# A decoder trunk on one core: the last block of a projection taken half by half, and the norm's reciprocal and spread in two pieces

## The chip, the core and the metric

The kernel runs on one core of a Trainium2 chip. The metric is the device time of one launch in microseconds. 2992.96 us is the median of 3 runs of the kernel before.

## What is computed

A step of a four-layer decoder trunk over 512 prompt tokens and 8 sample tokens, 520 columns in all, with a model width of 1024. Each layer has a token mixer (a gated short convolution, RWKV-7, gated linear attention, a short convolution again) and a gated feed-forward part with a convolution. Each of these eight sub-layers stands between two norms:

```
def rmsnorm(x, g, eps=RMS_EPS):
    xf = x.astype(jnp.float32)
    y = xf * lax.rsqrt(jnp.mean(xf * xf, axis=-1, keepdims=True) + eps)
    return (y * g.astype(jnp.float32)).astype(x.dtype)
...
        u = rmsnorm(h, p['norm_g'][l, 0]) * (1 + sc_m) + sh_m
...
        h = h + gt_m * rmsnorm(out, p['norm_g'][l, 1])
        u = rmsnorm(h, p['norm_g'][l, 2]) * (1 + sc_f) + sh_f
        out, nb = conv_ffn(u, st_conv_f[l], p['ffn_w_up'][l], p['ffn_conv_w'][l], p['ffn_conv_b'][l],
                           p['ffn_w_down'][l])
        new_f.append(nb)
        h = h + gt_f * rmsnorm(out, p['norm_g'][l, 3])
```

That is sixteen norms: eight ahead of a sub-layer (here "pre") and eight behind it ("post").

## The kernel before

Activations lie transposed: the 1024 features are eight tiles of 128 partitions, the 520 tokens are the columns. A projection is a row of blocks, each one output tile of 128 features. A block's accumulator `tile_ps[slot]` is two PSUM banks, one for each half of 260 tokens. Weights are split into a high and a low part so that products keep float32 accuracy: for each block SyncE loads `w_raw`, ScalarE writes `w_hi` (`high`, L1037), GpSimd writes `w_lo` (`low`, L814), and TensorE (`gemm`) takes, for all k, `w_hi` with the high and the low part of x (L1722), both halves in turn, and then, for all k, `w_lo` with the high part (L1730). It waits for `lo_done` only between the two. Two weight slots alternate, and `high` for a block waits until the block two before it is done. A block of the out phase has 8 tiles of k, 48 matmuls; a down block is three pieces with 8, 7 and 7 (`DOWN_K`), the last with 42.

The projections `out` and `down` end in a post norm. During them VectorE squares each finished tile and adds it up in `csb[:, 0]`; `sum_ready` says that all tiles but the last are in it. The last tile is squared by ScalarE straight from PSUM (`square_last`, L1100 and L1101, one instruction for a half), after the whole block is done, and then copied (`evacuate`, L1106, L1107). TensorE adds over features with a matrix of ones (`token_sums`, L1784), first `csb[:, 0]` and then the squares of the last tile. The result has 4 groups of rows, with 128 prompt columns each, and 8 sample columns: 136 columns. ScalarE takes the root (`root`, L1063), VectorE the reciprocal (`inverse_root`, L2641), and TensorE spreads it over all partitions (`spread_rstd`): L1826 is one product for the 8 sample columns, L1828 four products of 128 columns, float32. Each of these is two weight loads and two matmuls in the trace. VectorE then multiplies the eight tiles by it (`times_rstd`, L2695) and adds to `h` (L2751).

A pre norm squares `h` tile by tile on ScalarE (L1072) as the post norm finishes it, and goes on with the same root, reciprocal and spread. Of its eight, seven follow a post norm at once; the first is in the prologue, where TensorE also works on loads of `ada_pro`.

In six of the eight posts TensorE has other work, the modulation products of the next half layer (`ada_ahead`, L1683): four steps, 32 instructions, between `token_sums` and `spread_rstd`, and four more after. The posts at 2566 and 2971 us have none. All engines run queues in program order and wait for each other by semaphores, whose counts are written out by hand.

Of the kernel before, what the change touches and what calls it, by code (L numbers as in the profile page):

```python
# [16 lines left out]
ACT = mybir.ActivationFunctionType  # L17
# [7 lines left out]
HALF = T // 2  # L25
KT = D // P
DFF = 2816
FT = DFF // P
# [20 lines left out]
NG = 4  # L49
TG = T // NG  # L50
SPAN = 3 * TG
NW = TP // NG
# [19 lines left out]
def trunk_kernel(nc, A, O, depth):  # L72

    ctx = ExitStack()
    with ctx:
# [194 lines left out]
        def sem(name):  # L270
            return ctx.enter_context(nc.semaphore(name))
# [35 lines left out]
        usb_done = sem("usb_done")  # L307
        uhi_done, last_squared = sem("uhi_done"), sem("last_squared")
        u_ready = sem("u_ready")
        h_ready = sem("h_ready")  # L310
# [708 lines left out]
        def _(act):  # L1019
# [76 lines left out]
            def square_last(s, n, index):  # L1096

                act.wait_ge(sum_ready, index + 1)
                act.wait_ge(block_done, n + 3)
                act.activation(csb[:, 1, 0:HALF], tile_ps[s][0][:, 0:HALF], ACT.Square)  # L1100
                act.activation(csb[:, 1, HALF:T], tile_ps[s][1][:, 0:HALF], ACT.Square).then_inc(last_squared, 1)  # L1101
# [546 lines left out]
        def _(pe):  # L1648
# [65 lines left out]
            def gemm(n, s, slot, xh, xl, k0, nk, start, stop, ready=None, between=None):  # L1714
# [17 lines left out]
                return mm.then_inc(block_done, 1)  # L1732

            def gemm_pair(n, pre, xh, xl, ready, hi=(uhi_done, None), weights=(w_hi, w_lo), start=True, stop=True):

# [86 lines left out]
            def spread_rstd(norm):  # L1822

                pe.wait_ge(rstd_ready, norm + 1)
                row = lambda g: ident[:, g * QUAD:g * QUAD + 1].to_broadcast([P, P])
                pe.matmul(rstd_ps[1], row(NG - 1), rstd[:, NW:NGW], start=True, stop=True).then_inc(rstd_turned, 1)  # L1826
                for g in range(NG):
                    mm = pe.matmul(rstd_ps[0][:, g * NW:(g + 1) * NW], row(g), rstd[:, 0:NW], start=True, stop=True)  # L1828
                mm.then_inc(rstd_turned, 1)
# [27 lines left out]
            for p in plan:  # L1857
# [632 lines left out]
                elif p["kind"] == "out":  # L2490
                    xh, xl, ready, r0 = p["x"]

                    def out_block(it, e):

                        pe.wait_ge(tile_free[e], t0 // 2 + it + 1)
                        gemm(n0 + 2 * it + e, e, e, xh, xl, 0, KT, True, True, (ready, r0) if e == 0 else None)

# [13 lines left out]
                    if l % 3 == 2:  # L2511
                        for b in range(2 * p["iters"]):
                            out_block(b // 2, b % 2)
                            if b < NS // 2:
                                sample_products(b)
                    else:
                        first = 0
                        if l % 3 == 0:
                            out_block(0, 0)
                            turn_tails(p["conv"])  # L2520
                            out_block(0, 1)
                            first = 1
                        with pe.Fori(first, p["iters"]) as it:
                            for e in range(2):
                                out_block(it, e)
                elif p["kind"] == "up":
                    pe.wait_ge(std_done, p["norm"])
# [18 lines left out]
                elif p["kind"] == "down":  # L2546
# [3 lines left out]
                    def down_pair(it):  # L2550
                        for e in range(2):
                            pe.wait_ge(tile_free[e], t0 // 2 + it + 1)
                            for i, (k0, nk) in enumerate(DOWN_K):
                                k = 3 * e + i
                                gemm(n0 + 6 * it + k, k % 2, e, hid_hi, hid_lo, k0, nk, i == 0, i == 2,
                                     (hid_ready, p["unit"] - FT + k0) if e == 0 else None)
                                if it == 0 and k == 1:
# [27 lines left out]
        def _(dve):  # L2585
# [52 lines left out]
            def inverse_root(norm):  # L2638

                dve.wait_ge(std_done, norm + 1)  # L2640
                dve.reciprocal(rstd[:, 0:NGW], std[:, 0:NGW]).then_inc(rstd_ready, 1)  # L2641

# [624 lines left out]
```

## Time and profile before

| what | value |
|---|---|
| median of 3 runs | 2992.96 us (2991.05 to 2993.82) |
| the profiled execution | 2992.34 us |
| its span, first to last instruction | 2990.5 us |
| TensorE matmuls busy | 2845.7 us, 95% |
| weight loads busy | 2711.8 us, 91% |
| VectorE, ScalarE, GpSimd busy | 51%, 36%, 44% |
| mean granted TensorE clock | 0.975 of full |
| reciprocals L2641 | 16, 1.00 us each |

The busy shares are means over stages with different limits. For this change the stages between two projections matter, and there the order of starts in the timeline says who waits for whom. Matmuls are pipelined: each is shown some 0.27 us long while they follow each other every 0.11 to 0.12 us, so the distance between starts is what a matmul costs. For the weight loads (PEld) the same holds.

### The profile page before, as it was taken

The numbers are of one execution on the slowest core, as the hardware profiler recorded it, in microseconds if no ns is written. First come the engines' busy times: TensorE is split into PE (matmuls) and PEld (weight loads), VectorE is DVE, ScalarE is ACT, GpSimd is POOL, SyncE is SP. The second block draws the span as 40 slices with busy tenths as digits, with TensorE's granted clock in tenths as the row PEclk, the third lists the DMA queues.
The fourth block names the chain that finished last, engine by engine and source line by source line (L and its number), as shares of the span: only waits on it lengthen the run. The fifth ranks groups of instructions, "written<-read, shape, count | busy, mean of one in ns | idle before, by whom it ended". The sixth has DMA issues, their size and how long they took to land. (4 is left out here: it accounts for less than half of the span.)

```text
span 2990.5 us, 71312 instructions
## 1 busy us (share of the span) xinstructions
PE 2845.7 (95%) x29353; PEld 2711.8 (91%) x29353; DVE 1535.0 (51%) x2080; ACT 1062.6 (36%) x2047; POOL 1314.5 (44%) x957
## 2 busy tenths in 40 slices
PE   6999999998998999899999899999999999899998
PEld 5998999997988986899998799889999899799998
DVE  3445766117446885676603342476650444577612
ACT  3224333225455652433323543343332422433322
POOL 3443544442434563354443273434444344355443
PEclk8999999998999999999999999999999999899999
DMA  7544333444411004333344323533334543233332
GB/s 268 166 149 171 92 91 91 157 128 135 121 51 31 4 12 136 123 91 91 104 157 154 112 64 113 171 120 91 91 116 149 172 125 86 64 91 91 90 93 86
DMA packets 462286, 332.59 MB, mean 111 GB/s; under 512 B 16567, under 2 KB 432261, under 8 KB 461791
## 3 DMA queue, kind: packets, MB, share of 16 engines
q1 hardware_dynamic: 460148, 325.80, 35.2%
q10 hardware_dynamic: 1930, 3.68, 0.5%
q8 instruction: 172, 2.82, 0.4%
q14 instruction: 36, 0.29, 0.0%
HBM read 319.66 MB, written 10.20 MB: 110 GB/s over the span
## 5 line engine op out<-in xcount | busy, mean ns | idle before, releaser
L814 POOL TENSOR_TENSOR w_lo<-w_raw,w_hi 128x1024 fp32r<-128x1024 f32 x394 | 1005.0, 2551 | 1095.3 <-ACT w_hi L1037 1074.7
L1722 PE MATMUL banks<-u_hi,w_hi 128*128 128x260 f32 x4016 | 812.6, 283 | 18.9 <-ACT w_hi L1037 18.9
L1722 PE MATMUL banks<-u_lo,w_hi 128*128 128x260 f32 x4016 | 812.1, 283 | 0.0
L1722 PEld LDWEIGHTS banks<-u_hi,w_hi 128*128 128x128 f32 x4016 | 620.5, 189 | 29.4 <-issue 24.3
L1722 PEld LDWEIGHTS banks<-u_lo,w_hi 128*128 128x128 f32 x4016 | 621.6, 189 | 0.0
L1037 ACT ACTIVATE w_hi<-w_raw 128x1024 fp32r<-128x1024 f32 x402 | 424.6, 1057 | 463.9 <-PE banks L1730 296.7
L1730 PE MATMUL banks<-u_hi,w_lo 128*128 128x260 f32 x4016 | 520.7, 282 | 0.0
L1730 PEld LDWEIGHTS banks<-u_hi,w_lo 128*128 128x128 f32 x4016 | 497.0, 188 | 0.0
L1722 PE MATMUL banks<-hid_hi,w_hi 128*128 128x260 f32 x1664 | 336.4, 283 | 0.5 <-DVE hid_lo L2683 0.5
L1722 PE MATMUL banks<-hid_lo,w_hi 128*128 128x260 f32 x1664 | 335.1, 283 | 0.0
L3202 DVE TENSOR_TENSOR csb<-proj 128x520 f32 (+1 forms) x42 | 30.2, 719 | 470.2 <-ACT proj L1107 470.2
L2683 DVE TENSOR_TENSOR hid_lo<-prod,hid_hi 128x520 f32 x104 | 262.0, 2520 | 12.8
L1722 PEld LDWEIGHTS banks<-hid_hi,w_hi 128*128 128x128 f32 x1664 | 256.7, 188 | 5.7 <-issue 3.7
L1722 PEld LDWEIGHTS banks<-hid_lo,w_hi 128*128 128x128 f32 x1664 | 256.1, 188 | 0.0
L2667 DVE SCALAR_TENSOR_TENSOR conv<-gate,vecs,conv 128x536 f32<-128x536 f32 x104 | 246.9, 2374 | 15.1 <-DVE conv L2665 0.8
L1730 PE MATMUL banks<-hid_hi,w_lo 128*128 128x260 f32 x1664 | 217.0, 282 | 0.0
L1730 PEld LDWEIGHTS banks<-hid_hi,w_lo 128*128 128x128 f32 x1664 | 206.4, 188 | 0.0
L832 POOL TENSOR_TENSOR tails<-gate,ones 128x2 f32 (+1 forms) x104 | 29.2, 281 | 328.9 <-ACT gate L1595 328.9
L1602 ACT ACTIVATE conv<-conv,vecs 128x536 f32<-128x536 f32 x88 | 65.5, 744 | 288.2 <-DVE conv L2667 288.2
L1593 ACT ACTIVATE gate<-banks 128x260 f32<-128x260 f32 x88 | 34.1, 387 | 356.4 <-PE banks L1730 355.7
L2664 DVE TENSOR_SCALAR conv<-gate,vecs 128x536 f32<-128x536 f32 x104 | 57.9, 556 | 177.0 <-ACT gate L1595 173.0
L2665 DVE SCALAR_TENSOR_TENSOR conv<-gate,vecs,conv 128x536 f32<-128x536 f32 x104 | 113.8, 1095 | 15.2 <-DVE conv L2664 1.6
(471 smaller groups left out, 3840.0 us busy)
## 6 DMA issues: line engine op xcount, KB each, us to landing
w_raw<-in_ffn_w_up_dram SPq DMA_DIRECT2D x176, 512.0 KB, 3.7
ada_raw<-in_ada_w_dram SPq DMA_DIRECT2D x96, 512.0 KB, 4.7
w_raw<-in_ffn_w_down_dram SPq DMA_DIRECT2D x64, 448.0 KB, 3.7
w_raw<-in_sconv_w_in_dram SPq DMA_DIRECT2D x48, 512.0 KB, 5.0
ada_ahead<-in_ada_w_dram SPq DMA_DIRECT2D x36, 512.0 KB, 7.2
ada_ahead_down<-in_ada_w_dram SPq DMA_DIRECT2D x36, 512.0 KB, 5.9
w_raw<-in_ffn_w_down_dram SPq DMA_DIRECT2D x32, 512.0 KB, 4.0
ada_pro<-in_ada_w_dram SPq DMA_DIRECT2D x6, 2048.0 KB, 21.5
```

The source lines that it names most:

```text
L814: pool.tensor_tensor(w_lo[:, s, :, :], w_raw[:, s, :, :], w_hi[:, s, :, :].bitcast(F32), ALU.subtract).then_inc(lo_done, 1)
L832: pool.tensor_tensor(to[:, 0:2], gate[:, e, TP:TP + 2], ones[:, 0:2], ALU.mult).then_inc(pool_step, 1)
L1037: act.activation(w_hi[:, s, :, :], w_raw[:, s, :, :], ACT.Copy).then_inc(hi_done, 1)
L1593: act.activation(gate[:, e, 2:2 + HALF], tile_ps[0][0][:, 0:HALF], ACT.Copy)
L1602: act.activation(conv[:, e, 0:CWD], conv[:, e, 0:CWD], ACT.Silu, bias=vec("ffn_conv_b", l * FT + m)).then_inc(silu_done, 1)
L1722: pe.matmul(tile_ps[slot][half][:, 0:HALF], w_hi[:, s, k, :], x[:, k0 + k, half * HALF:(half + 1) * HALF], start=start and k == 0 and i == ...
L1730: mm = pe.matmul(tile_ps[slot][half][:, 0:HALF], w_lo[:, s, k, :], xh[:, k0 + k, half * HALF:(half + 1) * HALF], start=False, stop=stop an ...
L2664: link(dve.tensor_scalar(conv[:, e, 0:CWD], gate[:, e, 0:CWD], w[0], None, ALU.mult))
L2665: link(dve.scalar_tensor_tensor(conv[:, e, 0:CWD], gate[:, e, 1:1 + CWD], w[1], conv[:, e, 0:CWD], ALU.mult, ALU.add))
L2667: dve.scalar_tensor_tensor(conv[:, e, 0:CWD], gate[:, e, 2:2 + CWD], w[2], conv[:, e, 0:CWD], ALU.mult, ALU.add).then_inc(conv_done, 1)
L2683: dve.tensor_tensor(lo, prod[:, e, :], hi.bitcast(F32), ALU.subtract).then_inc(hid_ready, 1)
L3202: return dve.tensor_tensor(csb[:, 1, :], o, o, ALU.mult)
```

## The change

The last block of an `out` or `down` projection is computed by a new function, `gemm_halves`: all products of the first half of tokens, then all of the second. It waits for `hi_done` and `lo_done` before its first matmul. A new semaphore, `first_half_done`, is raised between the halves, and `square_last` squares the first half on it. The loops over output tiles run one iteration less on TensorE and the last one is written out. The reciprocal becomes two instructions, columns 64 to 135 first and then 0 to 63, and the four products of L1828 become eight with 64 columns each, the upper columns first, behind a wait for their piece.

```
             def square_last(s, n, index):
                 act.wait_ge(sum_ready, index + 1)
+                act.wait_ge(first_half_done, index + 1)
+                act.activation(csb[:, 1, 0:HALF], tile_ps[s][0][:, 0:HALF], ACT.Square)
                 act.wait_ge(block_done, n + 3)
-                act.activation(csb[:, 1, 0:HALF], tile_ps[s][0][:, 0:HALF], ACT.Square)
                 act.activation(csb[:, 1, HALF:T], tile_ps[s][1][:, 0:HALF], ACT.Square).then_inc(last_squared, 1)
...
+            def gemm_halves(n, s, slot, xh, xl, k0, nk, start):
+
+                pe.wait_ge(hi_done, n + 1)
+                pe.wait_ge(lo_done, n + 3)
+                for half in range(2):
+                    for k in range(nk):
+                        for w, x in ((w_hi, xh), (w_hi, xl), (w_lo, xh)):
+                            mm = pe.matmul(tile_ps[slot][half][:, 0:HALF], w[:, s, k, :],
+                                           x[:, k0 + k, half * HALF:(half + 1) * HALF],
+                                           start=start and k == 0 and w is w_hi and x is xh, stop=k == nk - 1 and w is w_lo)
+                    mm.then_inc(block_done if half else first_half_done, 1)
...
             def spread_rstd(norm):
-                pe.wait_ge(rstd_ready, norm + 1)
+                pe.wait_ge(rstd_ready, 2 * norm + 1)
                 row = lambda g: ident[:, g * QUAD:g * QUAD + 1].to_broadcast([P, P])
                 pe.matmul(rstd_ps[1], row(NG - 1), rstd[:, NW:NGW], start=True, stop=True).then_inc(rstd_turned, 1)
-                for g in range(NG):
-                    mm = pe.matmul(rstd_ps[0][:, g * NW:(g + 1) * NW], row(g), rstd[:, 0:NW], start=True, stop=True)
+                for part in (1, 0):
+                    pe.wait_ge(rstd_ready, 2 * norm + 2 - part)
+                    cols = slice(part * NW // 2, (part + 1) * NW // 2)
+                    for g in range(NG):
+                        out = rstd_ps[0][:, g * NW:(g + 1) * NW]
+                        mm = pe.matmul(out[:, cols], row(g), rstd[:, cols], start=True, stop=True)
                 mm.then_inc(rstd_turned, 1)
...
-                    def out_block(it, e):
+                    def out_block(it, e, final=False):
                         pe.wait_ge(tile_free[e], t0 // 2 + it + 1)
-                        gemm(n0 + 2 * it + e, e, e, xh, xl, 0, KT, True, True, (ready, r0) if e == 0 else None)
+                        if final and e:
+                            gemm_halves(n0 + 2 * it + e, e, e, xh, xl, 0, KT, True)
+                        else:
+                            gemm(n0 + 2 * it + e, e, e, xh, xl, 0, KT, True, True, (ready, r0) if e == 0 else None)
...
-                        with pe.Fori(first, p["iters"]) as it:
+                        with pe.Fori(first, p["iters"] - 1) as it:
                             for e in range(2):
                                 out_block(it, e)
+                        for e in range(2):
+                            out_block(p["iters"] - 1, e, True)
...
+                                if it == p["iters"] - 1 and k == 5:
+                                    gemm_halves(n0 + 6 * it + k, k % 2, e, hid_hi, hid_lo, k0, nk, False)
...
             def inverse_root(norm):
                 dve.wait_ge(std_done, norm + 1)
-                dve.reciprocal(rstd[:, 0:NGW], std[:, 0:NGW]).then_inc(rstd_ready, 1)
+                dve.reciprocal(rstd[:, NW // 2:NGW], std[:, NW // 2:NGW]).then_inc(rstd_ready, 1)
+                dve.reciprocal(rstd[:, 0:NW // 2], std[:, 0:NW // 2]).then_inc(rstd_ready, 1)
```

(`NG` is 4, `NW` 128, `NGW` 136, `HALF` 260.)

## Rows read from the trace of the kernel before

**Rows 1.** The page, parts 1 and 4 (busy time; chain that ended last)
```profile
PE 2845.7 (95%) x29353; PEld 2711.8 (91%) x29353; DVE 1535.0 (51%) x2080; ACT 1062.6 (36%) x2047; POOL 1314.5 (44%) x957
...
PE banks L1722 24%; PE banks L1730 12%; PE banks L2055 1%; PE banks L1683 1%; DVE h L2751 1%; PE banks L1745 1%; DVE proj L2695 1%; PE banks L1828 0%; PE banks L1784 0%; PE banks L1751 0%; PE banks L2006 0%; PE banks L2116 0%; PE banks L213
```

**Rows 2.** Timeline, post norm at 257: start, length, engine, line, operation, [idle before]
```profile
252.06 0.70 DVE L3228 TENSOR_TENSOR csb<-csb 128x520 f32<-128x520 f32 x1
...
256.43 0.39 ACT L1100 ACTIVATE csb<-banks 128x260 f32<-128x260 f32 x1 [4.19 <-PE banks L1730]
...
256.71 0.38 ACT L1101 ACTIVATE csb<-banks 128x260 f32<-128x260 f32 x1
...
257.14 0.44 PE L1784 MATMUL banks<-csb,ones 128*32 128x136 f32 x8 [0.45 <-ACT csb L1101]
...
257.40 1.91 PE L1683 MATMUL banks<-ada_ahead,cT 128*32 128x256 f32 x32
...
257.65 0.37 ACT L1063 ACTIVATE std<-banks,eps_col 128x136 f32<-128x136 f32 x1
...
258.13 1.00 DVE L2641 RECIPROCAL rstd<-std 128x136 f32<-128x136 f32 x1
...
259.24 0.30 PEld L1826 LDWEIGHTS banks<-rstd,ident 128*128 128x128 f32 x2 [0.41 <-DVE rstd L2641]
...
259.46 0.97 PEld L1828 LDWEIGHTS banks<-rstd,ident 128*128 128x128 f32 x8
...
260.73 1.29 DVE L2695 TENSOR_TENSOR proj<-proj,banks 128x512 f32<-128x512 f32 x2 [0.19 <-PE banks L1828]
```

**Rows 3.** Timeline of the pre norm at 274, TensorE and VectorE
```profile
274.58 0.39 PE L1826 MATMUL banks<-rstd,ident 128*128 128x8 f32 x2 [1.54 <-DVE rstd L2641]
...
276.05 0.69 DVE L2695 TENSOR_TENSOR prod<-h,banks 128x512 f32<-128x512 f32 x1 [0.83 <-PE banks L1828]
```

**Rows 4.** Timeline of the post norm at 2566, TensorE
```profile
2567.48 0.39 PE L1826 MATMUL banks<-rstd,ident 128*128 128x8 f32 x2 [1.60 <-DVE rstd L2641]
```

**Rows 5.** Timeline of the pre norm at 2581, weight loads of the spread
```profile
2582.45 1.83 PEld L1828 LDWEIGHTS banks<-rstd,ident 128*128 128x128 f32 x8
```

**Rows 6.** Windows: stretch, length, busy us of each engine, PEclk, DMA share, GB/s
```profile
2580.90:2590.10 9.20, 6.70 (x30) 6.38 (x31) 6.13 (x13) 4.79 (x8) 0.00 (x0) 0.50 0.01 2
...
2970.70:2972.40 1.70, 0.13 (x1) 0.13 (x2) 1.23 (x2) 0.41 (x2) 0.00 (x0) 1.00 0.00 0
```

**Rows 7.** Timeline: low parts of two last blocks, and the blocks before them
```profile
1204.75 2.90 POOL L814 TENSOR_TENSOR w_lo<-w_raw,w_hi 128x1024 fp32r<-128x1024 f32 x1 [2.83 <-ACT w_hi L1037]
...
1206.57 2.07 PE L1730 MATMUL banks<-u_hi,w_lo 128*128 128x260 f32 x16
...
2960.60 2.40 POOL L814 TENSOR_TENSOR w_lo<-w_raw,w_hi 128x1024 fp32r<-128x1024 f32 x1 [2.57 <-ACT w_hi L1037]
...
2962.55 1.83 PE L1730 MATMUL banks<-hid_hi,w_lo 128*128 128x260 f32 x14
```

**Rows 8.** Timeline of the post norms at 670 and 1942
```profile
668.35 1.06 ACT L1037 ACTIVATE w_hi<-w_raw 128x1024 fp32r<-128x1024 f32 x1 [9.86 <-DMA w_raw<-in_rwkv_w_dram]
...
1942.03 0.94 DVE L2739 TENSOR_TENSOR s<-proj_b,mod_m 128x64 f32<-128x64 f32 x1 [4.91 <-ACT proj_b L1107]
...
1944.06 0.39 PE L1826 MATMUL banks<-rstd,ident 128*128 128x8 f32 x2 [0.48 <-DVE rstd L2641]
```

**Rows 9.** Groups by line: two reciprocals; timeline: loads of L2055
```profile
L2641 DVE RECIPROCAL rstd<-std x16: 1002/1003/1005, 31.8 to 2971.2; 128x136 f32<-128x136 f32 x16
...
L3131 DVE RECIPROCAL rstd<-std x1: 966/966/966, 1138.6 to 1138.6; 128x130 f32<-128x130 f32 x1
...
1741.87 2.42 PEld L2055 LDWEIGHTS banks<-g_ex 128*128 128x128 f32 x21
```

**Rows 10.** Timeline of the prologue, TensorE
```profile
44.88 3.64 PE L1849 MATMUL banks<-ada_pro,cT 128*32 128x128 f32 x64 [3.28 <-DMA ada_pro<-in_ada_w_dram]
```

**Rows 11.** The core's span and mean granted clock
```profile
core 0: 2990.5 us, clock 0.975
```

More of the change, by code:

```diff
@@ L308, in trunk_kernel @@
         uhi_done, last_squared = sem("uhi_done"), sem("last_squared")
+        first_half_done = sem("first_half_done")
         u_ready = sem("u_ready")
@@ L2512, in _ @@
                         for b in range(2 * p["iters"]):
-                            out_block(b // 2, b % 2)
+                            out_block(b // 2, b % 2, b == 2 * p["iters"] - 1)
                             if b < NS // 2:
@@ L2554, in down_pair @@
                                 k = 3 * e + i
-                                gemm(n0 + 6 * it + k, k % 2, e, hid_hi, hid_lo, k0, nk, i == 0, i == 2,
-                                     (hid_ready, p["unit"] - FT + k0) if e == 0 else None)
+                                if it == p["iters"] - 1 and k == 5:
+                                    gemm_halves(n0 + 6 * it + k, k % 2, e, hid_hi, hid_lo, k0, nk, False)
+                                else:
+                                    gemm(n0 + 6 * it + k, k % 2, e, hid_hi, hid_lo, k0, nk, i == 0, i == 2,
+                                         (hid_ready, p["unit"] - FT + k0) if e == 0 else None)
                                 if it == 0 and k == 1:
```

## The prediction

> **What bounds the kernel now.** I read the page first. TensorE is busy for 95% of the span and the weight loads beside it for 91%, while no other engine passes 51%; the chain that ended last runs over L1722 and L1730, the projection matmuls [rows 1]. Time is made or lost where TensorE starves, and the norms are such places. So I then read the stages around the norms in the timeline, one by one; this change touches nothing else.
>
> A post norm begins when the last block of a projection ends. In the pattern that four posts show (at 257, 1215, 1624 and 2353 us) the reader should follow ScalarE first [rows 2]: the two squares start at 256.43 and 256.71, then two copies, then the root at 257.65. ScalarE works without a gap here, and TensorE's sums end at 257.58, so both allow the root at about the same moment. Then come the reciprocal (258.13 to 259.13), the small product L1826 at 259.24 and the eight loads of L1828 from 259.46. In these posts TensorE has 32 instructions of L1683 between sums and spread; they end about 259.3, so L1826 starts behind them, not behind the reciprocal, which was there some 0.05 us before. L2695 at 260.73, and all of the norm behind it, waits for L1828.
>
> A pre norm has nothing on TensorE between sums and spread: it idles 1.54 us for the reciprocal, L1826 starts at 274.58 and L2695 at 276.05 [rows 3]. Seven pres are on the path, six of them like this. The post at 2566 has no L1683 either, and idles 1.60 us [rows 4]; the post at 2971 is like it up to L1826. Two spreads met the lower level of the clock: from 2580.9 to 2590.1 the granted clock was 0.50, 1.2 GHz, and there the eight loads of L1828 took 1.83 us instead of 0.97; in the post at 2971 it was full until 2972.4 and half behind that, with L1828 wholly in the lower part [rows 2, 5, 6].
>
> **The wait for w_lo.** The last block now asks for w_lo before its first matmul. In an out phase w_lo is there at 1207.65 and the block before ends its matmuls at about 1208.6; in a down phase it is there at 2963.00, and the block before ends at 2964.4 [rows 7]. So 0.9 to 1.4 us of TensorE's work on the previous block hides it: 0; without that cover it would cost the 2.4 to 2.9 us of a low part. The order of the 48 (or 42) matmuls changes, not their number, and each already has a weight load of its own, so the block stays as long. That the last iteration leaves the loop costs nothing either: TensorE shows no idle time between two blocks in a loop or out of it.
>
> **The early square.** sum_ready comes at 252.76 [rows 2], the first half of the block is done halfway through its 5.7 us, at about 253.5, and ScalarE is free by then. The first square moves under the second half, and the second starts at 256.43 instead of 256.71. Copies, root, sums and L1683 all come 0.28 us earlier. This holds in seven of eight posts. At 670 both squares stand behind a w_hi that its DMA kept until 668.35, after the block's end: nothing there. In the post at 1942 VectorE's small multiply takes 0.94 us, to 1942.97, beside a low part of POOL that is not moved, and the reciprocal starts only behind it: nothing there [rows 8]. Six times 0.28 is -1.68 us.
>
> **The reciprocal in two pieces.** 136 columns take 1003 ns and 130 take 966 [rows 9]: 6.2 ns for a column and a fixed 0.16 us. The first piece, 72 columns, then takes about 0.606 us, the second 0.557, and L1826 can start 0.397 us earlier, where it waits for the reciprocal. It does in the seven pres, in the posts at 2566 and 2971, and in those at 670 and 1942, where the reciprocal starts late (L1826 at 1944.06, while L1683 had ended some 0.5 us before): 11 times -0.397 is -4.37 us. In the four posts of rows 2 L1683 hides it: 0. If a piece had no fixed part the gain would be 0.8 us more. The second piece ends about 1.2 us after the root, and the first eight loads run until 1.8, so its wait is hidden. The small multiply behind L1826 now stands behind the second piece on VectorE, with over half a microsecond to spare before L1828 ends.
>
> **The spread in two pieces.** This is the dear part. A product of L1828 is two weight loads and two matmuls; the eight loads take 0.97 us, (0.97 - 0.19) / 7 = 0.111 us apart [rows 2]. The new code has sixteen, with 64 columns each. Do 64 columns cost half? The nearest row says no: L2055 has the same type and weights and 64 columns, and 21 of its loads took 2.42 us, (2.42 - 0.19) / 20 = 0.1115 us apart [rows 9]. Even the two loads of L1826, for 8 columns, are 0.11 apart: 259.24 to 259.46 is 0.22 [rows 2]. The weights set the pace, not the columns. So a spread grows by 8 x 0.1115 = 0.892 us; at the lower clock the loads are (1.83 - 0.33) / 7 = 0.213 apart [rows 5], and it grows by 1.71.
>
> The Trainium skill (TensorE: Matmul & The Clock Gate, LDWEIGHTS) puts a load of 128 columns of weights at 128 / 1.2 = 107 ns; the trace agrees with 0.111. The table in Back-to-back issue gap of the same page counts about 60 cycles for up to 64 columns and 134 for 128. By that table alone sixteen would cost what eight did, and the time would be that of the second rival.
>
> Thirteen spreads at the full clock on the path: +11.60. The pre at 2581, at the lower one: +1.71. The post at 2971: its products now start 0.68 us earlier and find the clock full until about 2972.4, so some six loads go at 0.1115 and ten at 0.213; the spread then ends 0.44 us later than before, which is +1.12 beside its -0.28 and -0.40 above. The prologue's spread grows by 0.9 us ahead of an idle wait of 3.28 us for a DMA [rows 10]: hidden, 0.
>
> **The sum.** 11.60 + 1.71 + 1.12 - 1.68 - 4.37 = +8.4 us. By kind: a pre at full clock loses 0.50, a post with L1683 0.61, the post at 2566 0.21. All of it reaches the end, since L2695 follows L1828 at once and everything later in the norm follows L2695. The profiled execution took 2992.34 us (a span of 2990.5 and 1.8 around it), 0.6 below the median, so I lay the sum on the median: 2992.96 + 8.4 = 3001.4 us.
>
> **The rivals.**
> 1. *The clock takes another share.* A mean granted clock of 0.975 [rows 11] means 2 x 0.025 x 2990.5 = 150 us at the lower level. The norms move in time and in their idle gaps, so other stretches may fall low. A spread that falls low costs 0.8 us more; four more of them, and the pair of blocks behind them, some 5 us: 3006. The other way, both low spreads at full clock give back 1.1 us, and a few of the low microseconds elsewhere bring it to about 2998, within 0.2%. For it: the posts at 2566 and 2971 are alike up to L1826, and only the second met the low level, so small things decide. Against: TensorE gets more work in the norms, not less. Chance of 3005 and more 0.1, of landing within 0.2% 0.14.
> 2. *The columns set the pace after all*, the other side. If a product of 64 columns took half of one with 128, the spread would be as long as before and only the gains stay: 2992.96 - 1.68 - 4.37 = 2986.9. Where it decides: the 14.43 us of the spreads are 16.2 times 0.892, and 6.05 / 16.2 = 0.37, so the loads would have to be (0.892 + 0.37) / 16 = 0.079 us apart; below that the change is faster. For it: L1828 by itself shows only that a load and 128 columns together take 0.111 us, not which of them sets it. Against: L2055 and L1826. Chance 0.1.
> 3. *The longer spread is partly hidden* by VectorE's update of the sample columns, which in a post runs beside it. It ends about 0.2 us before L2695 starts, so nothing is hidden now and a longer spread only widens that; 3001 stays. It would need VectorE to be late by half a microsecond, in eight posts: 2997. Chance 0.05.
> 4. *The wait for w_lo bites* in some phases: 0.5 to 2.9 us a time, up to eight times, 3005 to 3020. Against it the margins of 0.9 and 1.4 us. Chance 0.03.
>
> **How the numbers follow.** The forecast has 0.58. Its own range, from the fixed part of the reciprocal (-0.8), the clock of the low spreads (-1.1, or +1.6 for two more) and the 1 to 2 us between runs, is 2998.5 to 3004.5. To hold 8 in 10 it reaches into the clock rival on both sides: 2996.5 to 3006.5. About 0.2%, 6 us, is what a measurement of this kernel can tell from no change; the forecast lies only 2.4 beyond it. Within 0.2%: the better half of rival 1, rival 3 and the forecast's low end, 0.2. Faster: rival 2, 0.1. Slower: 0.7.
>
> **What the changed profile would show.** Twice as many spread products, 64 columns each, their loads still 0.11 us apart and some 1.85 us in a row; at 0.06 apart rival 2 holds. Reciprocals of about 0.61 and 0.56 us. The second square just behind the last matmul, the first some 2.5 us before it. From L1826 to L2695: 1.47 us before, about 2.36 after. The prediction is wrong if that distance does not grow, if the last block of a projection shows an idle wait for w_lo, or if the stretches at the lower clock sum to much more or less than 150 us.

## The result and the profile after

The changed kernel took 2996.61 us (median of 22 runs, 2991.29 to 3007.84) beside 2991.30 us for the kernel before on the same chip (22 runs). The ratio is 1.0018, 95% interval 1.0011 to 1.0025: 5.4 us more (3.3 to 7.5). The forecast was 8.4 more, 3001.4 us. That is 4.8 us above what was measured: 3.0 of it is the size of the change, the rest the kernel before, whose median over 22 runs is 1.7 below that of the 3 runs that the forecast stood on. The profiled execution took 2997.98 us, with a span of 2996.3 at a mean granted clock of 0.975, the same clock as before. The lines of the profile after are 1 to 27 higher: `gemm_halves` is L1743, the squares L1101 and L1103, the root L1064, the reciprocals L2667 and L2668, the small product L1840, the spread L1846, `times_rstd` L2722.

The post norm at 258, which answers to [rows 2], in the timeline:

```profile
254.75 0.39 ACT L1101 ACTIVATE csb<-banks 128x260 f32<-128x260 f32 x1 [1.33 <-PE banks L1743]
...
257.25 0.28 PE L1743 MATMUL banks<-hid_hi,w_lo 128*128 128x260 f32 x1
...
257.57 0.39 ACT L1103 ACTIVATE csb<-banks 128x260 f32<-128x260 f32 x1 [2.43 <-PE banks L1743]
...
258.51 0.37 ACT L1064 ACTIVATE std<-banks,eps_col 128x136 f32<-128x136 f32 x1
...
258.99 0.60 DVE L2667 RECIPROCAL rstd<-std 128x72 f32<-128x72 f32 x1
259.51 0.49 DVE L2668 RECIPROCAL rstd<-std 128x64 f32<-128x64 f32 x1
...
260.10 0.30 PEld L1840 LDWEIGHTS banks<-rstd,ident 128*128 128x128 f32 x2 [0.41 <-DVE rstd L2668]
...
260.32 1.86 PEld L1846 LDWEIGHTS banks<-rstd,ident 128*128 128x128 f32 x16
...
260.78 0.62 DVE L2770 TENSOR_TENSOR h<-h,s 128x64 f32<-128x64 f32 x1
...
262.43 0.69 DVE L2722 TENSOR_TENSOR proj<-proj,banks 128x512 f32<-128x512 f32 x1 [1.03 <-PE banks L1846]
```

The first square starts 2.50 us ahead of the last matmul, the second 0.04 behind its end. From the last matmul's end (257.53) to the end of the root (258.88) it is 1.36 us unrounded; before it was 1.70. Sixteen loads take 1.86 us, (1.86 - 0.19) / 15 = 0.111 apart, with 64 columns as with 128. The last matmul's end to the first L2722 is 4.90 us, to L2695 before it was 4.40.

A pre norm at the full clock, which answers to [rows 3], and the price of the two pieces in the groups by line:

```profile
1228.56 0.60 DVE L2667 RECIPROCAL rstd<-std 128x72 f32<-128x72 f32 x1 [1.64 <-ACT std L1064]
...
1229.22 0.39 PE L1840 MATMUL banks<-rstd,ident 128*128 128x8 f32 x2 [1.13 <-DVE rstd L2667]
...
1229.46 1.98 PE L1846 MATMUL banks<-rstd,ident 128*128 128x64 f32 x16
...
1231.53 0.69 DVE L2722 TENSOR_TENSOR prod<-h,banks 128x512 f32<-128x512 f32 x1 [1.67 <-PE banks L1846]
```

```profile
L2667 DVE RECIPROCAL rstd<-std 128x72 f32<-128x72 f32 x16 | 9.7, 603 | 21.2 <-ACT std L1064 20.4
L2668 DVE RECIPROCAL rstd<-std 128x64 f32<-128x64 f32 x16 | 7.9, 495 | 0.0
```

TensorE waits 1.13 us for the first piece where it waited 1.54 [rows 3], and L2722 then waits 0.84 longer for the spread. From L1840 to L2722 it is 2.31 us, where L1826 to L2695 was 1.47.

The wait for w_lo at the last out block, and the pre at 2585, which met the lower clock as before [rows 5], in the timeline:

```profile
1202.20 2.90 POOL L815 TENSOR_TENSOR w_lo<-w_raw,w_hi 128x1024 fp32r<-128x1024 f32 x1 [3.05 <-ACT w_hi L1038]
...
1205.94 0.28 PE L1743 MATMUL banks<-u_hi,w_hi 128*128 128x260 f32 x1
...
2586.25 3.53 PEld L1846 LDWEIGHTS banks<-rstd,ident 128*128 128x128 f32 x16
...
2590.07 0.69 DVE L2722 TENSOR_TENSOR prod<-h,banks 128x512 f32<-128x512 f32 x1 [3.34 <-PE banks L1846]
```

w_lo is there at 1205.10, 0.84 us before the block's first matmul; in the eight last blocks the margin is 0.84 to 1.23, and no two matmuls in them start more than 0.13 apart. A block of 48 matmuls takes 5.92 us from start to end, where it took 5.91. The loads at the lower clock are (3.53 - 0.33) / 15 = 0.213 apart.

The post at 1942, where ScalarE, VectorE and GpSimd set the time, answers to [rows 8]:

```profile
1940.00 1.06 ACT L1038 ACTIVATE w_hi<-w_raw 128x1024 fp32r<-128x1024 f32 x1 [4.44 <-DMA w_raw<-in_ffn_w_up_dram]
1940.97 0.37 ACT L1101 ACTIVATE csb<-banks 128x260 f32<-128x260 f32 x1
...
1942.27 1.33 DVE L2766 TENSOR_TENSOR s<-proj_b,mod_m 128x64 f32<-128x64 f32 x1 [5.17 <-ACT proj_b L1109]
1943.63 0.60 DVE L2667 RECIPROCAL rstd<-std 128x72 f32<-128x72 f32 x1
```

Here a w_hi whose DMA landed late keeps both squares until 1940.97, 0.37 us behind the last matmul; the early square does not happen, and the root is 0.25 us later than before. The small multiply takes 1.33 us where it took 0.94, so the reciprocal starts 0.63 later.

Adding up one stage at a time gives the difference by place. A norm's stage goes, in a post, from the end of the last projection matmul to L2722 (L2695 before), in a pre from the end of the root to it. Profiled execution after minus before:

| stages | us |
|---|---|
| four posts with L1685 behind the sums, 0.50 each | +2.0 |
| posts at 670, 1942, 2566, 2971 | -1.13, +1.07, +0.94, +0.40 |
| pres at 1230, 1640, 1957, 0.44 each | +1.3 |
| pres at 274, 688, 2370, whose spreads met the lower clock in part | +2.7 |
| pre at 2581, lower clock in both | +1.2 |
| sum of the norms' stages | +8.5 |
| from the pres' L2722 to the first projection matmul: 274, 688, 2370 | +1.2, -0.7, +1.1 |
| projections up to the next post: behind the pres at 274 and 688 | -2.5, -2.3 |
| all else | +0.4 |
| span | +5.7 |

The rows below the sum of the norms are for the most part the clock's share: outside the norms' stages the time at the lower level, added up from the clock's record in the trace, is 135.2 us after and 145.0 before. The windows show the two largest terms, first before and then after, for the stretches from the projection behind the pre at 274 to the end of its down phase, and behind the pre at 688:

```profile
278.06:667.39 389.33, 386.56 (x3249) 383.42 (x3251) 194.85 (x210) 120.75 (x214) 180.32 (x110) 1.00 0.36 108
695.37:1214.37 519.00, 485.14 (x8578) 440.22 (x8582) 329.31 (x609) 256.98 (x660) 231.38 (x265) 0.97 0.22 62
```

```profile
281.73:668.53 386.80, 384.81 (x3249) 381.70 (x3250) 193.83 (x208) 120.40 (x213) 180.63 (x110) 1.00 0.36 110
695.09:1211.85 516.76, 481.27 (x8579) 436.48 (x8582) 331.20 (x609) 257.39 (x661) 232.12 (x265) 0.98 0.22 63
...
274.50:278.40 3.90, 2.76 (x30) 2.50 (x23) 1.24 (x3) 0.38 (x1) 0.00 (x0) 0.87 0.03 8
```

The same number of matmuls, and 2.5 and 2.2 us less. In the second pair the time at the lower level is 20.5 us in place of 34.1. The last row is the pre at 274 after the change: the end of its spread and the modulation products behind it (L1685) fell low, from 277.4 to 280.8, and neither did before. In the first pair the clock is only part of it. Before, 3.4 us from 293.0 on were at the lower level and cost 1.6 us; after, none were. Of the other 1.0 us, 0.8 is a shorter wait for w_hi ahead of that stretch, first before and then after:

```profile
292.74 0.58 PE L1722 MATMUL banks<-u_hi,w_hi 128*128 128x260 f32 x2 [2.77 <-ACT w_hi L1037]
...
295.40 0.48 PE L1724 MATMUL banks<-u_hi,w_hi 128*128 128x260 f32 x2 [1.99 <-ACT w_hi L1038]
```

That w_hi ends 16.55 us behind L2695 before and 16.72 behind L2722 after, so it does not follow the modulation products on TensorE. Of the 1.2 us that those lost by falling low, all but 0.2 are given back by the time this matmul starts.

Where the clock's record is the same, most short stretches between norms agree to 0.01 us between the two profiles. The two long ones in which neither profile has any time at the lower level, up to the posts at 1624 and 2566, differ by +0.16 and -0.33.

### The profile page after: what moved, and what is told of

It reads as the page before. It is cut to its first block and busy times, and to the rows that moved or that the text cites. A ratio compares the mean times of both kernels' runs of the same rounds, so it can differ in the third digit from the quotient of the medians.

```text
span 2996.3 us, 71570 instructions
## 1 busy us (share of the span) xinstructions
PE 2860.9 (95%) x29481; PEld 2725.2 (91%) x29481; DVE 1544.1 (52%) x2096; ACT 1063.6 (35%) x2047; POOL 1314.1 (44%) x957
## 5 line engine op out<-in xcount | busy, mean ns | idle before, releaser
L1724 PE MATMUL banks<-hid_hi,w_hi 128*128 128x260 f32 x1576 | 318.8, 284 | 1.4 <-ACT w_hi L1038 0.9
L1724 PE MATMUL banks<-hid_lo,w_hi 128*128 128x260 f32 x1576 | 317.5, 283 | 0.0
L1724 PEld LDWEIGHTS banks<-hid_hi,w_hi 128*128 128x128 f32 x1576 | 243.2, 189 | 6.8 <-issue 3.7
L1724 PEld LDWEIGHTS banks<-hid_lo,w_hi 128*128 128x128 f32 x1576 | 242.5, 188 | 0.0
L1732 PE MATMUL banks<-hid_hi,w_lo 128*128 128x260 f32 x1576 | 205.5, 282 | 0.0
L1732 PEld LDWEIGHTS banks<-hid_hi,w_lo 128*128 128x128 f32 x1576 | 195.5, 188 | 0.0
L1595 ACT ACTIVATE gate<-banks 128x260 f32<-128x260 f32 x88 | 34.1, 387 | 353.3 <-PE banks L1732 352.8
```

The costliest lines, as they stand in the source:

```text
L1595: act.activation(gate[:, e, 2:2 + HALF], tile_ps[0][0][:, 0:HALF], ACT.Copy)
L1724: pe.matmul(tile_ps[slot][half][:, 0:HALF], w_hi[:, s, k, :], x[:, k0 + k, half * HALF:(half + 1) * HALF], start=start and k == 0 and i == ...
L1732: mm = pe.matmul(tile_ps[slot][half][:, 0:HALF], w_lo[:, s, k, :], xh[:, k0 + k, half * HALF:(half + 1) * HALF], start=False, stop=stop an ...
```

## The experiments

Each kernel was compared with the kernel before on the same chip; the edits shown are against the changed kernel. In the kernels with block and squares as before, the last iteration still stands outside its loop. The ratio on record is not quite that of the two medians: for the spread alone 3008.82 beside 2990.05 is 1.0063, 18.8 us, and for the change once more 2992.54 beside 2992.28 is 1.0001. "Norms" is the sum of the norms' stages against the profile of before, taken as above from one profiled execution. It leaves out what the clock does elsewhere, so it tells small edits apart where the medians can't. There is one profile of before, and its post at 670, which a DMA kept, is 7.12 us long; in the twelve others it is 4.65 to 6.43. That difference is not the edits' and is in every sum, so the next column leaves this post out.

| kernel | ratio (95%) | in us of 2991 | norms, us | without 670 | mean clock |
|---|---|---|---|---|---|
| the change | 1.0018 (1.0011 to 1.0025) | +5.4 | +8.5 | +9.7 | 0.975 |
| the change, once more | 1.0008 (0.9999 to 1.0018) | +2.4 | +6.3 | +7.0 | 0.979 |
| first edit | 0.9992 (0.9983 to 1.0001) | -2.4 | -3.1 | -0.9 | 0.974 |
| first edit, again | 0.9978 (0.9968 to 0.9989) | -6.6 | -3.0 | -0.9 | 0.978 |
| first edit, semaphore as before | 0.9969 (0.9958 to 0.9980) | -9.3 | -4.1 | -2.1 | 0.978 |
| the same, again | 0.9981 (0.9972 to 0.9991) | -5.7 | -4.1 | -2.1 | 0.978 |
| reciprocal in two | 0.9984 (0.9975 to 0.9993) | -4.8 | -5.3 | -3.0 | 0.979 |
| spread in two | 1.0068 (1.0054 to 1.0081) | +20.3 | +16.2 | +17.0 | 0.974 |
| first edit, reciprocal in two | 0.9979 (0.9970 to 0.9988) | -6.3 | -7.4 | -5.0 | 0.980 |
| the same, again | 0.9983 (0.9973 to 0.9993) | -5.1 | -7.2 | -4.9 | 0.978 |
| reciprocal and spread in two | 1.0020 (1.0011 to 1.0029) | +6.0 | +10.3 | +11.2 | 0.979 |
| rows of 32 in seven posts | 0.9971 (0.9962 to 0.9980) | -8.7 | -9.4 | -6.9 | 0.975 |

**The first edit alone.** The last block half by half with the early square; one reciprocal, which raises the semaphore by two, and the spread whole:

```
-                dve.reciprocal(rstd[:, NW // 2:NGW], std[:, NW // 2:NGW]).then_inc(rstd_ready, 1)
-                dve.reciprocal(rstd[:, 0:NW // 2], std[:, 0:NW // 2]).then_inc(rstd_ready, 1)
+                dve.reciprocal(rstd[:, 0:NGW], std[:, 0:NGW]).then_inc(rstd_ready, 2)
...
-                for part in (1, 0):
-                    pe.wait_ge(rstd_ready, 2 * norm + 2 - part)
-                    cols = slice(part * NW // 2, (part + 1) * NW // 2)
-                    for g in range(NG):
-                        out = rstd_ps[0][:, g * NW:(g + 1) * NW]
-                        mm = pe.matmul(out[:, cols], row(g), rstd[:, cols], start=True, stop=True)
+                pe.wait_ge(rstd_ready, 2 * norm + 2)
+                for g in range(NG):
+                    mm = pe.matmul(rstd_ps[0][:, g * NW:(g + 1) * NW], row(g), rstd[:, 0:NW], start=True, stop=True)
```

> Only the first edit: the last block half by half and its first half squared early; one reciprocal of 136 columns, one spread of eight loads. My theory: the early square is a small true gain, the moved order of matmuls and the early wait for w_lo are free. The root ends 0.3 us earlier after the last matmul in six posts, the distance from the root's end to L2695 stays at 2.57 (pre) and 2.70 (post with modulation work): -1.7 to -2.4 us, ratio 0.9993. Rival (the block in the new order, or its wait for w_lo, is what costs): slower by 3 to 5 us, and the last block longer than 5.7 us or with an idle wait ahead of it.

It took 2987.98 us, 2.4 less than before. The posts with work between sums and spread gain 0.34 us each, and no last block waits. The pre shows something else, in the timeline:

```profile
272.63 0.37 ACT L1064 ACTIVATE std<-banks,eps_col 128x136 f32<-128x136 f32 x1 [1.48 <-PE banks L1798]
...
273.10 1.00 DVE L2664 RECIPROCAL rstd<-std 128x136 f32<-128x136 f32 x1 [2.64 <-ACT std L1064]
```

The reciprocal starts 0.10 us behind the root's end, not 0.03, and L1843, the spread, 0.07 later with it. That is a cost of this experiment, 0.07 by 11, and not of the change.

**The reciprocal alone.** Block and squares as before, two reciprocals, the spread whole behind the second:

```
-                for part in (1, 0):
-                    pe.wait_ge(rstd_ready, 2 * norm + 2 - part)
...
+                pe.wait_ge(rstd_ready, 2 * norm + 2)
+                for g in range(NG):
```

> Only the reciprocal in two pieces (about 0.60 and 0.50 us, 0.52 apart); the last block and the squares as before; the small product after the first piece, then the four products of 128 columns after the second. My theory: two pieces end 0.02 to 0.05 us later than one, but the small product's two loads (0.22 us) are now done before the second piece is ready, so the spread starts about 0.2 us earlier where it waited for the reciprocal (11 norms) and not in the four posts with modulation work: about -2 us, ratio 0.9993. Rival (splitting the reciprocal itself costs, by its fixed part): +0.1 to 0.2 us a norm, +1.5 to 3 us.

2985.66 us, 4.8 less. The pre in the timeline:

```profile
273.10 0.60 DVE L2659 RECIPROCAL rstd<-std 128x72 f32<-128x72 f32 x1 [1.64 <-ACT std L1064]
273.62 0.49 DVE L2660 RECIPROCAL rstd<-std 128x64 f32<-128x64 f32 x1
273.76 0.30 PEld L1839 LDWEIGHTS banks<-rstd,ident 128*128 128x128 f32 x2 [1.41 <-DVE rstd L2659]
...
274.17 0.97 PEld L1842 LDWEIGHTS banks<-rstd,ident 128*128 128x128 f32 x8
```

The small product hides under the second piece, and the eight loads start 0.41 us behind it, not 0.22. So even with the spread behind both pieces, L2714 comes 0.21 us earlier in a pre. In the four posts with L1684 it is 2.70 us behind the root, as before: hidden there, as predicted. Of the -5.3 in the norms' stages 2.3 are the post at 670 and 0.6 the one at 1942, which here is as long as those four and was longer before. The 2.5 that are left are near the 2 that I had expected.

**The spread alone.** Block and squares as before, one reciprocal raising by two, the sixteen products of the change:

```
-                dve.reciprocal(rstd[:, NW // 2:NGW], std[:, NW // 2:NGW]).then_inc(rstd_ready, 1)
-                dve.reciprocal(rstd[:, 0:NW // 2], std[:, 0:NW // 2]).then_inc(rstd_ready, 1)
+                dve.reciprocal(rstd[:, 0:NGW], std[:, 0:NGW]).then_inc(rstd_ready, 2)
```

> Only the spread in sixteen loads of 64 columns, behind one reciprocal of 136; the last block and squares as before. My theory (a load of 128 columns of weights sets the pace): the spread is longer by 0.84 us in each of 15 norms on the path, more at the lower clock, nothing is given back: +12 to +15 us, ratio 1.0045, loads 0.111 us apart. Rival 2 of the prediction (columns set the pace): 0. Rival clock (the loss comes from which stretches fall to the lower level, not from the spread): the ratio is near that of the full change, 1.0018, and root to L2695 hardly grows.

3008.82 us, 1.0068: 20.3 us more. The timeline at 274 and at 1642:

```profile
275.97 1.86 PEld L1845 LDWEIGHTS banks<-rstd,ident 128*128 128x128 f32 x16
276.00 1.98 PE L1845 MATMUL banks<-rstd,ident 128*128 128x64 f32 x16
...
1643.44 0.39 PE L1839 MATMUL banks<-rstd,ident 128*128 128x8 f32 x2 [1.60 <-DVE rstd L2662]
1643.66 3.27 PEld L1845 LDWEIGHTS banks<-rstd,ident 128*128 128x128 f32 x16
...
1647.21 0.69 DVE L2716 TENSOR_TENSOR prod<-h,banks 128x512 f32<-128x512 f32 x1 [3.13 <-PE banks L1845]
```

```profile
1642.50:1647.50 5.00, 4.06 (x26) 3.71 (x29) 1.40 (x3) 0.00 (x0) 0.00 (x0) 0.64 0.00 0
```

At the full clock a post loses 0.84 us. A pre loses 0.90 (L2716 3.47 us behind the root, for 2.57), because here too one reciprocal raises by two and starts 0.07 later. The norms' stages lose 16.2 in all, more than the 12 to 15 that I had written: four spreads that ran full before fell to the lower level, of which this one, with 3.27 us of loads at a mean granted clock of 0.64, is the longest. This settles the second rival: the dear part is the spread and nothing else, and 64 columns cost what 128 do.

**The first two edits, the spread whole.** The change with the eight products of before:

```
-                for part in (1, 0):
-                    pe.wait_ge(rstd_ready, 2 * norm + 2 - part)
...
+                pe.wait_ge(rstd_ready, 2 * norm + 2)
+                for g in range(NG):
```

> The whole change but for the spread: half by half, early square, reciprocal in two pieces, and four products of 128 columns as before. My theory: the two gains add up, about -4 us, ratio 0.9986 (0.9980 to 0.9993); root to L2695 is 2.36 in a pre instead of 2.57. Rival (the loss of the change does not sit in the spread): still slower than before, 1.001 or more.

2983.15 us, 0.9979, and 0.9983 in the run that is quoted further down: faster than the kernel before. In a pre L2719 is 2.35 us behind the root, against 3.00 in the change and 2.56 before. The mean of the two ratios, 0.9981, against 1.0013 for the change in its two runs, prices the pieces of the spread at 0.0032, 9.6 us. In the norms' stages it is 8.5 + 7.4 = 15.9 in one pair of profiles and 6.3 + 7.2 = 13.5 in the other (14.7 and 11.9 without the post at 670).

**The change without the first edit.**

```
                 act.wait_ge(sum_ready, index + 1)
-                act.wait_ge(first_half_done, index + 1)
-                act.activation(csb[:, 1, 0:HALF], tile_ps[s][0][:, 0:HALF], ACT.Square)
                 act.wait_ge(block_done, n + 3)
+                act.activation(csb[:, 1, 0:HALF], tile_ps[s][0][:, 0:HALF], ACT.Square)
...
-                        if final and e:
-                            gemm_halves(n0 + 2 * it + e, e, e, xh, xl, 0, KT, True)
```

> The change without its first edit: reciprocal and spread in two pieces, the last block and the squares as in the kernel before. My theory: the parts add up, so it stands above the full change by what the early square gives, 0.33 us in seven posts: about +7.5 us against the kernel before, ratio 1.0025 (1.0015 to 1.0040). Rival (the parts depend on each other: the early square only pays where the spread is whole): same as the full change, 1.0018 or less.

2996.70 us, 1.0020. Beside it the change itself ran once more:

> The full change on the same chip as the three above. From the first comparison (1.0018) and from the sum of the parts: 1.0010 to 1.0030. If the parts add up it is e4_both minus 2.3 us; if the spread alone carries the loss it stands 10 to 14 us above e7_halves_recip.

2992.54 us, 1.0008. The difference, 0.0012 or 3.6 us, has the sign of the first edit and is near its local price, but is no larger than what two runs of one kernel differ by.

**The first edit with the semaphore as before.** To see whether the 0.07 us come from the count:

```
-                pe.wait_ge(rstd_ready, 2 * norm + 1)
+                pe.wait_ge(rstd_ready, norm + 1)
...
+                dve.reciprocal(rstd[:, 0:NGW], std[:, 0:NGW]).then_inc(rstd_ready, 1)
```

> The first edit alone once more, but with the reciprocal and its semaphore exactly as in the kernel before. In e1_halves the one reciprocal raised its semaphore by two, and in its profile it started 0.10 us after the root instead of 0.03. If that step comes from the raise by two, it is gone here: reciprocal 0.03 us after the root, L2695 2.57 us after it in a pre, and the time about 0.8 us below e1_halves, ratio 0.9990. Rival (it came from something else in the first edit): the reciprocal starts 0.10 us after the root again.

The pre in the timeline:

```profile
272.11 0.37 ACT L1064 ACTIVATE std<-banks,eps_col 128x136 f32<-128x136 f32 x1 [0.56 <-PE banks L1798]
...
272.52 1.00 DVE L2663 RECIPROCAL rstd<-std 128x136 f32<-128x136 f32 x1 [1.64 <-ACT std L1064]
```

The reciprocal is back at 0.03 us behind the root. The time was a surprise: 2982.88 us, 0.9969, which is 9.3 us less where the norms' stages give 4.1, and 0.0023 below the first edit with the raise by two. So both, and the kernel with the first two edits, ran once more on one chip.

> The first edit alone, the reciprocal and its semaphore as before: the same kernel as the run that measured 9.3 us less (ratio 0.9969). If the early square's local price is all there is (8 norms by 0.33 us, about 2.7 us), this run gives 0.9991 (0.9982 to 1.0000) and the 9.3 us were the clock or the layout of that one program load. If the gain belongs to the program itself, it gives 0.9969 again, and the profile must have a stage outside the norms that is shorter by 5 us or more.

> The first edit with the reciprocal raising its semaphore by two, as in the first batch (0.9992). The later start of the reciprocal (0.07 us by 11) makes 0.8 us between this and the kernel with the semaphore as before. Beside it on the same chip: 0.0003 above that one's ratio if only this counts; 0.002 or more above it if the difference between the two kernels is real and is not in the norms.

> The first two edits, the spread whole: 0.9979 before. The reciprocal in two pieces is worth 0.21 to 0.28 us in 11 norms, 2.3 to 3.1 us, so this run should lie 0.0008 to 0.0010 below the kernel with the first edit alone; if it lies at or above it, then a few us between builds come from outside the edits, and the sizes of all small differences here are no better known than that.

They gave 0.9981, 0.9978 and 0.9983, with medians of 2985.04, 2984.19 and 2985.04 us. The order of the first two has turned round, and the three intervals overlap almost wholly. The gain of 9.3 us does not belong to the program. One kernel's ratio moves by 0.0004 to 0.0014 between two such comparisons, 1 to 4 us, more than its interval says. The sums over the norms' stages repeat better: -3.1 and -3.0, -4.1 and -4.1, -7.4 and -7.2. For the change itself they do not, with +8.5 and +6.3, mostly because its spreads and posts met the lower clock, a DMA and GpSimd differently. And all are taken against the one profile of before. By the expectation for the last one the two reciprocals should have shown as 0.0008 to 0.0010 between the medians; they show in the stages (3 to 4 us) and not in the medians.

**Rows of 32.** A row of `ident` picks one group of 32 partitions. In the posts but for the last, each product takes the 32 partitions alone and writes a bank of its own; the first two edits stay, and the pres keep the spread of before:

```
+                part_row = lambda g: ident[g * QUAD:(g + 1) * QUAD, g * QUAD:g * QUAD + 1].to_broadcast([QUAD, P])
...
+                            mm = pe.matmul(wide[:, g, cols], part_row(g), rstd[g * QUAD:(g + 1) * QUAD, cols], start=True, stop=True)
```

> e7_halves_recip and one thing more: in seven posts each of the four products takes only its own 32 rows of the weights and of the reciprocal (the others are zeros), into a bank of its own, and L2695 reads four banks. Theory A: loads that touch different rows run beside each other, as the 32-column loads of the sums do, so the eight take about 0.5 us instead of 0.97: -0.4 us in seven posts, -3 us against e7_halves_recip, ratio to the kernel before 0.9970. Theory B: the time of a load goes by its 128 columns whatever its rows, and all stand in one queue: the eight stay 0.11 us apart, ratio as e7_halves_recip, 0.9979.

2983.99 us, 0.9971. The post at 257 in the timeline:

```profile
259.32 0.31 PEld L1848 LDWEIGHTS banks<-rstd,ident 32*128 32x128 f32 x8
259.33 0.50 PE L1848 MATMUL banks<-rstd,ident 32*128 32x128 f32 x8
259.43 0.22 DVE L2780 TENSOR_TENSOR s<-s,banks 128x64 f32<-128x64 f32 x1 [0.53 <-PE banks L1841]
259.69 0.62 DVE L2781 TENSOR_TENSOR h<-h,s 128x64 f32<-128x64 f32 x1
...
260.34 1.28 DVE L2733 TENSOR_TENSOR proj<-proj,banks 128x512 f32<-128x512 f32 x2
```

Eight loads of 32 rows take 0.31 us in place of 0.97, the spread 0.50 in place of 1.14. The Trainium skill (TensorEngine Tiling (Array Packing), Key Properties) says that different tiles can load weights and multiply in parallel; the trace agrees: four loads with rows of their own start 0.007 us apart. Each product has two loads, though, and the second four follow the first 0.11 us later, so what runs side by side are the four products and not the two loads of one; the mean over all eight is (0.31 - 0.19) / 7 = 0.017 us. But L2733 now has no wait in front of it: it stands behind VectorE's own update of the sample columns (L2781, to 260.31), and starts 2.55 us behind the root where it was 2.70. The spread was shortened by 0.64 us, and 0.15 of it arrived in this post. In the posts at 1618 and 2559, L2733 comes 0.45 and 0.54 us earlier than without rows of 32. That gives -9.4 in the norms' stages against -7.3 without it; in the medians it lies 0.0008 to 0.0012 below the two runs without it, which is within what they vary.

## Why the prediction came out as it did

The direction was right and the range from 2996.5 to 3006.5 held the time, but by 0.1 us, and that is luck: the narrower range that the prediction gave for its own mechanism, 2998.5 to 3004.5, did not hold it, nor does the wide one hold the 2992.54 of the change once more. The prediction also drew a line at 0.2%, gave 0.7 to slower than that and 0.2 to what lies within it. The ratio is up by 0.18% (0.11 to 0.25), so by the middle value the less likely outcome came. Step by step:

**What bounds the norms**: right. L2722 follows the last product of the spread within 0.11 us in all fifteen norms on the path, and what the spread loses arrives behind it undiminished. Rival 3 (hidden by VectorE) is refuted here: the update of the sample columns ends at 261.40 in the post at 258, 1.0 us before L2722. It becomes true only when the spread is made short, as in the last experiment.

**The wait for w_lo**, 0: right, with margins of 0.84 to 1.23 us. Rival 4 is refuted.

**The early square**, -0.28 by 6: a small miss of size. It is -0.34, because the second square also follows the end of the block more closely, 0.04 us behind the last matmul where the first stood 0.10 behind it; why, no run tells. At 670 the squares stood behind a w_hi and its DMA again, as predicted, and did not come early. The stage there still got 1.13 us shorter, but it got 0.97 shorter in the kernel without the early square too: in each later profile the wait for that DMA is shorter than it was in the profile of before. That is no effect of the early square. At 1942 the prediction expected nothing because VectorE is late there; in this profile the squares were not early either, but 0.27 us late behind a w_hi. Its premise that the low part of POOL is not moved there did not hold: it starts at 1941.14, where it started at 1940.52, and the small multiply beside it takes 0.39 us more. In the change once more the first square started 0.8 us ahead of the end of the block, and this post took 4.90 us, as the four others.

**The reciprocal**, -0.397 by 11: right. The pieces take 603 and 495 ns. The first was forecast at 606; the second, at 557, was not, and it starts 0.08 us before the first ends, so a second piece costs 0.49 us and hides wholly. L1840 starts 0.40 earlier.

**The spread**, +0.892 by 13: right in its mechanism, mis-sized by 0.05. The loads do take 0.89 longer (1.86 for 0.97), but L2722 waits for the last matmul, and that one has 64 columns now and is shorter: 1.98 for 1.14 is 0.84. The table of gaps for short matmuls in the Trainium skill (TensorE: Matmul & The Clock Gate, Back-to-back issue gap) is for matmuls without their weight loads, as the lines above it there say, and does not describe this line: the trace has 0.111 us for a load and its matmul at 8, 64 and 128 columns, and the measurement decides. Rival 2 is refuted by that and by the 20.3 us of the spread alone.

**The sum.** With these sizes it is 13 by 0.84 = 10.9, 1.6 for the pre at 2581 (1.20 and its reciprocal's 0.40), about 1.1 for the last post, less 4.4 and 2.0: +7.2 in place of +8.4. The profile has +8.5 in the norms' stages: three spreads and the post at 2566 fell low in part (+2.2), the post at 1942 waited 0.6 longer than costed (its reciprocal started 0.63 later), and the post at 670 gave back 1.6. That this comes so near to the forecast's 8.4 is chance.

**The clock**, rival 1, is where most of the rest of the miss is. The forecast took the clock's share as unchanged; both directions of the rival came at once. Spreads fell low, and behind three of them the modulation products (not the pair of blocks, as the rival had it). From L2722 to the first projection matmul that is +1.2 at 274 and +1.1 at 2370; at 688 it is -0.7, for there TensorE had waited 1.76 us for VectorE's xb_lo before and has no wait now. Stretches of projections elsewhere spent less time low (-2.5 and -2.3, 0.8 of it a shorter wait for w_hi). So "all of it reaches the end" holds for what moves L2722, and not for what TensorE alone loses behind it. That the clock's record differs is shown. That the change itself causes the smaller share elsewhere is not, since two profiles of one and the same changed kernel have 148.6 and 126.7 us at the lower level, and those of all kernels here lie between 122 and 156. Which of the two one launch gets, and why, stays open. The 5.4 and 2.4 us by the ratios stand to 8.5 and 6.3 in the norms' stages with 3 to 4 us less each time, and so does the kernel without the first edit (6.0 to 10.3), while the spread alone has 4 more. Of these sums the post at 670 gave back 1.1 to 1.7 us that are not the edits', and one profile of before can't tell whether it is so long in every launch. With a repeat worth 1 to 4 us, I would not read more into it.

## What to carry to other kernels

Splitting a product by columns so as to start it earlier doubles its weight loads: count loads by the spacing of the nearest line in the trace, whatever its column count, and split only what starts at least that much earlier (here 0.40 us bought with 0.84). Splitting the elementwise instruction ahead of it is nearly free, since the second piece runs under whatever needs only the first, and it can be kept without the other; the same holds for the early square. Where effects are a few microseconds in three milliseconds, sum the stages of the profile between fixed instructions, look for the stages that a DMA or the clock lengthened in either profile, and run the same kernel twice before believing a ratio's interval.

## What was not expected of the hardware

- A reciprocal that raises its semaphore by two starts 0.10 us behind the root in a pre norm, by one 0.03: 2.63 against 2.57 us from root to `times_rstd` at the full clock, in two profiles each of the first edit.
- Two VectorE instructions in a row overlap: the second reciprocal starts 0.52 us behind the first, which is shown 0.60 long.
- Four float32 products of 32 rows, each in its own bank, are eight loads in two groups of four: 0.007 us apart in a group, the groups 0.11 apart. Eight loads of 128 rows are 0.111 apart each.
- Time at the lower level of TensorE's clock differs by up to 34 us between kernels that differ in a few instructions, and by 22 us between two runs of one kernel (148.6 and 126.7).
